# A two-model transformer kernel on one core: order of the wide products, one split moved, delta-rule and differential work moved to ScalarE

## What is computed

```python
def swiglu(x, wg, wu, wd):      # FFN: gate and up products, then the down product
    return (silu(x @ wg) * (x @ wu)) @ wd
def rms_norm(x, g):
    return x * lax.rsqrt(mean(x * x, axis=-1) + NORM_EPS) * g
def l2_norm(x):
    return x * lax.rsqrt(sum(x * x, axis=-1) + NORM_EPS)
# delta rule: q, k are l2-normed, v is weighted by beta = sigmoid(...)
rhs = concatenate([vc * bc[..., None], kb * exp(gc)[..., None]], axis=-1)
# differential mixer: h = rms_norm(x, g); q, k, v are columns of h @ w_in
```

## Time and profile before

| | us |
|---|---|
| median of 3 runs | 2373.32 (2372.55 to 2375.32) |
| the profiled execution, whole | 2373.28 |
| its span, first to last instruction | 2371.5 |
| TensorE (PE) busy | 2332.8 (98%) |
| weight loads (PEld) busy | 2060.6 (87%) |
| VectorE (DVE) busy | 1577.4 (67%) |
| ScalarE (ACT) busy | 1141.3 (48%) |
| mean granted TensorE clock | 0.999 of 2.4 GHz |

### The profile page before, as it was taken

How to read it: one execution, slowest core, us unless ns; L and a number is a source line. 1 busy time by engine, 2 the same in 40 slices (tenths; PEclk the granted TensorE clock), 3 DMA queues, 4 the chain that set the end, 5 groups by cost and what they waited for, 6 DMA issues and landing times. The chain is left out here.

```text
span 2371.5 us, 39200 instructions
## 1 busy us (share of the span) xinstructions
PE 2332.8 (98%) x16836; PEld 2060.6 (87%) x16836; DVE 1577.4 (67%) x2151; ACT 1141.3 (48%) x1473; POOL 153.0 (6%) x177
## 2 busy tenths in 40 slices
PE   9999999999999999999999999999999999999998
PEld 8888888888889888899988899888998888998887
DVE  5566775666575865668665657766677656877665
ACT  5444744434435644455553445534465434655432
POOL 0100000020000000011210000100001001021000
PEclk9999999999999999999999999999999999999999
DMA  7766355656656366454265644556445565433662
GB/s 243 245 210 139 108 179 194 207 176 223 208 141 161 123 207 202 155 150 126 73 202 189 213 154 143 178 195 205 157 143 177 184 207 155 139 109 108 204 208 94
DMA packets 320828, 405.13 MB, mean 171 GB/s; under 512 B 48720, under 2 KB 281264, under 8 KB 320656
## 3 DMA queue, kind: packets, MB, share of 16 engines
q1 hardware_dynamic: 314992, 383.50, 51.2%
q0 software_dynamic: 5664, 19.13, 2.6%
HBM read 401.55 MB, written 1.05 MB: 170 GB/s over the span
## 5 line engine op out<-in xcount | busy, mean ns | idle before, releaser
L468 DVE TENSOR_TENSOR w_lo<-raw,w_hi 128x2048 fp32r<-128x2048 f32 (+1 forms) x355 | 799.2, 2275 | 58.4 <-ACT w_hi L461 58.0
L461 ACT CAST w_hi<-raw 128x2048 fp32r<-128x2048 f32 (+1 forms) x355 | 671.6, 1892 | 301.1 <-PE ps L484 231.9
L512 PE MATMUL ps<-aT,w_hi 128*128 128x512 f32 x2048 | 718.8, 398 | 0.0
L514 PE MATMUL ps<-aT,w_lo 128*128 128x256 f32 x1792 | 502.8, 281 | 0.0
L512 PEld LDWEIGHTS ps<-aT,w_hi 128*128 128x128 f32 x2048 | 374.2, 188 | 72.8
L514 PEld LDWEIGHTS ps<-aT,w_lo 128*128 128x128 f32 x1792 | 338.5, 189 | 10.0
L482 PE MATMUL ps<-w_hi,h_hi 128*128 128x512 f32 x864 | 339.2, 393 | 5.4 <-DVE h_lo L718 4.6
L484 PE MATMUL ps<-w_hi,h_lo 128*128 128x512 f32 x864 | 336.4, 389 | 0.0
L483 PE MATMUL ps<-w_lo,h_hi 128*128 128x512 f32 x864 | 336.4, 389 | 0.0
L482 PE MATMUL ps<-w_hi,aT 128*128 128x256 f32 (+2 forms) x992 | 300.5, 303 | 7.0 <-DVE aT L909 3.8
L484 PE MATMUL ps<-w_hi,aT 128*128 128x256 f32 (+2 forms) x992 | 294.1, 296 | 0.0
(11 more groups left out here) (397 smaller groups left out, 2787.3 us busy)
## 6 DMA issues: line engine op xcount, KB each, us to landing
raw<-in_mlp_w SPq DMA_DIRECT2D x124, 1024.0 KB, 5.3
raw<-in_ffn_wg SPq DMA_DIRECT2D x43, 1024.0 KB, 5.3
raw<-in_ffn_wu SPq DMA_DIRECT2D x43, 1024.0 KB, 5.3
raw<-in_ffn_wd SPq DMA_DIRECT2D x40, 1024.0 KB, 4.9
raw<-in_gdn_w_in SPq DMA_DIRECT2D x32, 1024.0 KB, 5.8
raw<-in_mlstm_w_in SPq DMA_DIRECT2D x12, 1024.0 KB, 5.4
raw<-in_diff_w_in SPq DMA_DIRECT2D x12, 1024.0 KB, 5.2
raw<-in_w_in SPq DMA_DIRECT2D x8, 1024.0 KB, 5.1
```

What stands on the lines that cost most here:

```text
L461: nc.scalar.copy(used_part(hi_slot(n), n), used_part(raw_slot(n), n)).then_inc(hi_ready, 1)
L468: nc.vector.tensor_tensor(used_part(lo_slot(n), n), used_part(raw_slot(n), n), used_part(hi_slot(n), n).bitcast(F32), ALU.subtract).then_i ...
L512: last = nc.tensor.matmul(ps[:, bank + ft, :], hi[:, k, c], aT[:, k, :], start=k == 0, stop=k == KT - 1)
L514: nc.tensor.matmul(ps[:, bank + ft, 0:SEQ], lo[:, k, c], aT_hi[:, k, :], start=False, stop=False)
```

## The change

Five edits. In `wide_product` the 8 wide matmuls of a block come in a row, the 8 narrow ones behind them; the matmuls are the same. In `ffn_vector` the first of the two splits behind the last gate (chunk 32) goes ahead of the add of the gate's halves. In the delta-rule mixer `v_turned` goes from `before` to `middle`, behind `right`, and `v_scaled` goes from one VectorE instruction per piece to four on ScalarE, which wait behind the split of the unit. The squares of the queries become four ScalarE instructions per piece that sum as they go (`accum_out`), so that VectorE's four `square_sums` of the queries fall away, and the step that adds epsilon to them (`square_sums_set(1)`) goes behind a split. In the differential mixer (q = 4) the tokens' factor is no longer in the turning: TensorE transposes H, and `projected` scales by `rs2` in two ScalarE instructions of 128 x 256 in place of one copy of 128 x 512.

```diff
@@ wide_product
-                last = nc.tensor.matmul(ps[:, bank + ft, :], hi[:, k, c], aT[:, k, :], start=k == 0, stop=k == KT - 1)
-                if k < KT - 1:
-                    nc.tensor.matmul(ps[:, bank + ft, 0:SEQ], lo[:, k, c], aT_hi[:, k, :], start=False, stop=False)
-                if k == KT - 2:
-                    nc.tensor.matmul(ps[:, bank + ft, 0:SEQ], lo[:, k + 1, c], aT_hi[:, k + 1, :], start=False, stop=False)
+                nc.tensor.matmul(ps[:, bank + ft, :], hi[:, k, c], aT[:, k, :], start=k == 0, stop=False)
+            for k in range(KT):
+                last = nc.tensor.matmul(ps[:, bank + ft, 0:SEQ], lo[:, k, c], aT_hi[:, k, :], start=False, stop=k == KT - 1)
@@ ffn_vector
+            ahead = split_ahead(FFN_ORDER, u)
+            if (kind, s) == ("gate", FF_STEPS - 1):
+                split_low(dve, n0 + ahead.pop(0))
...
-            for c in split_ahead(FFN_ORDER, u):
+            for c in ahead:
@@ weighted_x, token_factors
+    def factor_behind(q):
+        return q == 4
-        nc.vector.tensor_tensor(H[:, t, :], x[:, t, :], pre_g, ALU.mult)
+        last = nc.vector.tensor_tensor(H[:, t, :], x[:, t, :], pre_g, ALU.mult)
+        if factor_behind(q):
+            last.then_inc(pre_done.sem, 1)
...
     def token_factors(dve, q, t=0):
+        if factor_behind(q):
+            return
@@ diff_scalar, projected
-            nc.scalar.copy(dst, ps[:, u % 2, :].rearrange("p (t c) -> p t c", t=TT)).then_inc(df_act.sem, 1)
+            for t in range(TT):
+                act.wait_ge(pre_rs.sem, pre_rs.count(i, t))
+                last = nc.scalar.activation(dst[:, t, :], ps[:, u % 2, t * CW:(t + 1) * CW], ACT.Copy, scale=rs2[:, t:t + 1])
+            last.then_inc(df_act.sem, 1)
@@ gdn_tensor, before and middle
-            if 9 <= u <= 12:
-                v_turned(u - 9)
...
             if 10 <= u <= 14:
                 right(u - 9)
+            if 9 <= u <= 12:
+                v_turned(u - 9)
@@ gdn_scalar
+            done(gd_tn, 4 + e)
+            for t in range(TT):
+                for a in range(2):
+                    h = 2 * (e - 4) + a
+                    last = nc.scalar.activation(token_squares(e)[:, t, a, :], tokens[:, t, a, :], ACT.Square,
+                                                accum_out=g_r[:, 0, t, h:h + 1])
+            last.then_inc(gd_sq.sem, 1)
+        def v_scaled(c):
+            done(gd_tn, 4 + c)
+            done(gd_D, 0)
+            done(gd_ss, 3)
+            for t in range(TT):
+                for a in range(2):
+                    h = 2 * c + a
+                    last = nc.scalar.activation(g_v[:, t, h, :], ps[:, 3, (2 * t + a) * P:(2 * t + a + 1) * P], ACT.Copy,
+                                                scale=g_beta[:, t, h:h + 1])
+            last.then_inc(gd_vc.sem, 1)
...
+            if 8 <= u <= 11:
+                v_scaled(u - 8)
             if 7 <= u <= 14:
                 activate(u - 3)
@@ gdn_vector
-            if 13 <= u <= 15:
-                square_sums(u - 9)
-            if 8 <= u <= 11:
-                v_scaled(u - 8)
...
-                square_sums(7)
-                square_sums_set(1)
                 attention_set(0)
                 split_low(dve, n0 + 18)
+                square_sums_set(1)
                 split_low(dve, n0 + 19)
@@ prenorm_edge
-        return dict(xpass=xpass, src=H, scaled=True, ...
+        return dict(xpass=xpass, src=H, scaled=not factor_behind(q), ...
```

More of the change, by code:

```diff
@@ L2590, in two_block_model @@
                                                                gp("decays", TT))
-    gd_sq, gd_ss, gd_ssx, gd_r = gp("squares", 8), gp("square_sums", 8), gp("square_sums_set", 2), gp("norms", 2)
+    gd_sq, gd_ss, gd_ssx, gd_r = gp("squares", 8), gp("key_square_sums", 4), gp("square_sums_set", 2), gp("norms", 2)
     gd_tn, gd_kc, gd_vc = gp("chunk_turned", 12), gp("k_copied", 4), gp("v_scaled", 4)
@@ L2959, in squares @@
         def squares(e):
+            tokens = ps[:, 4 + e if e < 4 else 3, :].rearrange("p (t a v) -> p t a v", t=TT, v=P)
             if e < 4:
                 done(gd_tn, e)
[L2964 to L2969, removed]
+                nc.scalar.activation(token_squares(e), tokens, ACT.Square).then_inc(gd_sq.sem, 1)
+                return
+            done(gd_tn, 4 + e)
[15 more added lines that the diff above has]
+            last.then_inc(gd_vc.sem, 1)
         def k_copied(c):
@@ L3115, in square_sums @@
             done(gd_sq, e)
-            nc.vector.tensor_reduce(g_r[:, 1 - e // 4, :, 2 * (e % 4):2 * (e % 4) + 2], token_squares(e), AX.X,
-                                    ALU.add).then_inc(gd_ss.sem, 1)
+            nc.vector.tensor_reduce(g_r[:, 1, :, 2 * e:2 * e + 2], token_squares(e), AX.X, ALU.add).then_inc(gd_ss.sem, 1)
         def square_sums_set(a):
-            done(gd_ss, 4 * a + 3)
+            if a:
+                done(gd_sq, 7)
+            else:
+                done(gd_ss, 3)
             c = 16 - 16 * a
@@ L3182, in keys_decayed @@
             nc.vector.tensor_tensor(g_kbe[:, t, :, :], g_k[:, t, :, :], each(g_bre[:, t, :]), ALU.mult).then_inc(gd_kbe.sem, 1)
-        def v_scaled(c):
-            done(gd_tn, 4 + c)
-            nc.vector.tensor_tensor(g_v[:, :, 2 * c:2 * c + 2, :], ps[:, 3, :].rearrange("p (t a v) -> p t a v", t=TT, v=P),
-                                    g_beta[:, :, 2 * c:2 * c + 2].unsqueeze(3).to_broadcast([P, TT, 2, P]), ALU.mult).then_inc(gd_vc.sem, 1)
         def reads_copied(t):
@@ L3316, in prenorm_edge @@
                         half_ready=lambda pe, t, half: pe.wait_ge(mlp_w.sem, mlp_w.count(q // 2, 2 * t + half)))
-        return dict(xpass=xpass, src=H, scaled=True, early=False, fill={} if q else {(0, None): 3, (1, None): 8}, ready=lambda pe, t: pe.wait_ge(pre_done.sem, pre_done.count(q // 2, t)))
+        return dict(xpass=xpass, src=H, scaled=not factor_behind(q), early=False, fill={} if q else {(0, None): 3, (1, None): 8}, ready=lambda pe, t: pe.wait_ge(pre_done.sem, pre_done.count(q // 2, t)))
     def order_of_stages():
```

## The result

The changed kernel takes 2361.07 us (median of 4 runs, 2360.35 to 2361.90), beside 2373.18 for the kernel before in the same comparison: a ratio of 0.9946, 95% interval 0.9930 to 0.9961. So 12.1 us came where 16.5 were forecast. The profiled execution has a span of 2358.6 us, 12.9 less than before.

What follows compares the result with a forecast made beforehand. The prediction took TensorE, busy 98% of the span at full clock, as the bound. Savings of 8.0 + 5.2 + 2.4 + 0.9 = 16.5 us from 2373.3 gave 2356.8 us, range 2351.5 to 2365.

Steps and rivals of the forecast that it cites:

- rival C: Delta-rule wait only moves (0 for 2.4), half the FFN wait returns, 1 us lost to ScalarE: 2362.8 us, chance 0.13.
- Part 1: Wide products: sorting wide and narrow matmuls shortens blocks from 2.82 or 2.81 us to 2.79 or 2.77, saving 8.0 us.
- Rivals A: Wide products: a matmul costs the same in any company, so the new order gives nothing; 2364.8 us, chance 0.14.
- B: Wide products: wide matmuls stay slow, narrow ones lose their quick start, the order loses 3.4 us; 2368.2 us, chance 0.06.
- D: Wide products: narrow matmuls in a row outrun their weight loads, 25.6 us lost at 0.135 us each; 2390.4, chance 0.03.
- Part 2: End of each of four FFNs: the moved split removes TensorE's whole wait for `h_lo`, saving 5.2 us.
- Part 3: Two delta-rule mixers: the SiLU wait of 2.09 us goes, later waits take some back; 1.2 us per mixer, 2.4 won.
- the named waits: Delta-rule mixer, unit 10: TensorE waits 0.8 us at `right(1)` for copies of `g_T`, then at `both(1)` for `right_set`.
- what is late next: Delta-rule mixer: after the SiLU wait goes, `right(1)` awaits `g_T` copies and `both(1)` awaits `right_set`, leaving 1.2 us won.
- Part 4: Differential mixer: plain turning is 0.9 us shorter per tile row; won at the second turning only, 0.9 us in all.
- the half of the FFN wait: FFN ends, in rival C: half of the removed wait returns, so the moved split gives 2.6 us for 5.2.
- the loss to ScalarE: In rival C: 1 us lost to ScalarE.

Runs made afterwards that it cites:

- the pairs with the fetches out of the way: With against without the delta-rule edits: weights of 15 chunks per mixer loaded to an eighth (2357.11, 2361.23 us), or loads held back on the kernel before (2369.70, 2372.80).
- held_and_lam: Changed kernel, delta-rule weights loads of units 10 to 15 held until the small matmuls finish, lambda exp put behind the first two scaled copies: 2356.45 us.
- gdn_only: The kernel before with the delta-rule edits alone: median 0.8 us above the kernel before, ratio 1.0004.
- without_gdn: The changed kernel with its delta-rule edits taken back: 9.5 us quicker than the kernel before, ratio 0.9956.
- the four parts run alone: The kernel before with one part each: wide-product order 6.5 us less, moved split 5.0 less, delta-rule edits 0.8 more, differential edit the same in its median.
- before_held: The kernel before with the delta-rule weights loads of units 10 to 15 held back until the small matmuls finish: 2372.80 us.
- ffn_only: The kernel before with only the split moved ahead of the last gate's sum: 5.0 us less between the medians.

## Why the prediction was right and where it was not

The time lay in the range and the sign was right, but the measured 2361.07 is nearer to rival C (2362.8) than to the forecast (2356.8), and for a reason that neither named.

**Part 1** was right in its mechanism and almost in its size. Foreseen were blocks of 2.79 and 2.77 us, measured are 2.793 and 2.766, and the blocks alone give 8.4 us for the 8.5 foreseen. The slow first wide ones (233, 236, 228, 232, 231 ns, then 227) and the quick first narrow one (113, then 119 and 120) are there. The mis-sized term is the down products behind a block, put at 0.5 us "since they start slow now too". In before only their first step was slow (233, then 227); now it is the same row of five as above, and 24 of them take 5.468 us in place of 5.448: 80 x 0.020 = 1.6 us. That leaves 6.8 of 8.0. It was within the bound given (0.024 each). Rivals A, B and D are out, the last by narrow ones at 0.120.

The estimate of 107 ns a load that was weighed against this edit, from the Trainium skill, "TensorE: Matmul & The Clock Gate", "LDWEIGHTS (loading the stationary operand)", would have left next to no room for a load behind a narrow matmul. In after narrow ones in a row, a load with every one, take 0.120 us each, at most 0.007 more than the first behind a wide one.

**Part 2** was right in its mechanism: the wait is gone four times, and nothing came back. It gave 5.8 for 5.2. The rest is in the restart: the matmul behind the wait was followed by the next after 0.34 us (183.44 to 183.78 in before), not 0.23, and the working had counted only up to its start.

**Part 3** is where the forecast failed. Its own steps hold: the named waits stand at the named places (0.78 for 0.8 foreseen, 0.27 for 0.3), and with no late fetch the first mixer gains 1.20 us for 1.2. The costs on ScalarE were rightly put at nothing; four instructions of `v_scaled` take 1.14 us for 1.2. Timeline of ScalarE in after:

```profile
1085.66 1.14 ACT L2996 ACTIVATE ws<-ps,small 128x128 f32<-128x128 f32 x4
```

The step that failed is the question "what is late next". I asked it of ScalarE and VectorE and not of TensorE's own supply of instructions, though the trace of before had the hint, a wait put down to issue in the second mixer, at the edge of a packet that had started 2.45 us earlier. (The one in the earlier trace rows is that at the head of `both(1)` and no late fetch.) Among TensorE's waits in before:

```profile
PE ps L483 <- issue: 1.3, 1, 1.3
```

In the first mixer three late fetches took 2.6 us of start to start, more than was won. In the second, after had 0.94 and 0.23 where before had 1.56, so there it came out near the forecast's 1.2 by chance. I also missed what speaks for the edit: the wait that it removes could cost a stretch at half the clock. By the pairs with the fetches out of the way the edits are worth 3.1 to 4.1 us, not 2.4: 1.2 to 1.3 a mixer as forecast, and the rest, as far as the profiles tell, the falls of the clock. In the kernel as it is they earn part of that.

**Part 4** gave 0.33 for 0.9. The second turning won its time: the stretch around it is 0.99 us shorter. 0.4 came back at the third projection, by the queue behind the lambda exp, as held_and_lam shows; I had looked at ScalarE's load over the mixer ("free half of the time") and not at what stands ahead of these copies in its queue. Another 0.25 came back at the mixer's end, where TensorE's wait for VectorE grew as much; I did not test that one.

Rival C was right that the delta rule would bring nothing in gdn_only and in the first trace of after (+1.67 and -1.23), though not beside the other edits by the ratio of without_gdn. It was wrong in the cause, in the half of the FFN wait, and in the loss to ScalarE; that the time came near to its own is chance.

What stays open: why the start of the kernel and single blocks vary by up to a microsecond or two between executions; why the delta-rule edits win nothing alone and 2.4 to 3.3 us beside the others, so that the four parts run alone add up to 10.5 us and not to 12.1 or more; and how much of held_and_lam's gain another placement of the loads would reach. The best version run is held_and_lam, 0.9922 (0.9910 to 0.9934) of the kernel before.

## What to carry to other kernels

Before a wait is taken away, ask what the waiting engine gets its instructions from: where TensorE works through hundreds of tiny matmuls beside a large transfer, look for waits put down to issue and for the packets of the instruction queue, and place the large loads beside the large matmuls. A wait of about 2 us on TensorE can cost more than its length. And one profiled execution can hide or invent 3 us in such a stage, so compare starts stretch by stretch over several kernels before you price an edit from it.

## What the runs showed of the hardware

The fetch of TensorE's instructions shares the DMA engines with the weights and can be too late. The Trainium skill, "Runtime: NRT & Kernel Launch", "Instruction fetch mechanics", says that instructions come in blocks of 16 KiB, 256 of them, over a DMA queue of the sequencer's own; the 16 KB packets and the 257 instructions for each of them agree. It calls the cost of crossing a boundary mostly hidden. Here it is hidden in the six undisturbed cases above, where the packet starts 3.6 us or more ahead, and where a 1 MB load delays the packet, TensorE is idle for 0.2 to 1.3 us, once for 3.1 (gdn_only).

TensorE's granted clock fell to its lower level, 1.2 GHz, at 5 of 14 waits of 2.1 us. The fall came between 0.2 us before work began again (1093.18 and 1093.41 in before_held) and 1.3 us after it (1088.40 and 1087.14 in ffn_only), and cost 1.4 to 1.5 us each. In gdn_only it fell behind the late fetch of 3.06 us as well, 0.5 us after work had begun again.

A wide matmul's pace hangs on the width of those before it: 227 ns among its like, 228 to 236 for the first five behind narrow ones; a narrow one takes 120 ns, and 113 right behind a wide one. Alternating the two, as before did, costs 2.82 us a block, 0.03 more than sorting them.
